# A macaron block on one core: the sample stage in another order, a LayerNorm inside attention, and the third norm beside the output projection

## What is computed

```python
s1, sc1, g1, s2, sc2, g2, s3, sc3, g3 = ada(c)                 # shift, scale, gate per sequence
h = x + 0.5 * g1 * swiglu(modulate(x, g_ffn1, s1, sc1), ...)   # first feed-forward block
z = modulate(h, g_mix, s2, sc2) @ w_in      # conv GLU, q, k, v, index q/k, head weights, two gates
u = glu(z)                                  # prompt: zeros before it; samples: 30 rows of state before it
y = silu(layernorm(depthwise_conv(u, w_dw, 31 taps) + b_dw)) @ w_conv_out
att = sparse_attend(q, top-256 keys by index score) @ w_attn_o # samples: top 65 of 2 cache pages + 4 new keys
h = h + g2 * ((sigmoid(g_c) * y + sigmoid(g_a) * att) @ w_out) # mix and output projection
h = h + 0.5 * g3 * swiglu(modulate(h, g_ffn2, s3, sc3), ...)   # third norm, second feed-forward block
out = rmsnorm(h), k, v, index k, the conv state, for prompt and samples
```

## Time and profile before

| | us |
|---|---|
| median of 3 runs | 2858.69 (2857.79 to 2860.6) |
| profiled execution | 2858.35, its span 2856.2 |
| TensorE busy | 2616.9 (92% of the span) |
| VectorE busy | 1420.9 (50%) |
| ScalarE busy | 595.0 (21%) |
| GpSimd busy | 932.1 (33%) |
| HBM read, written | 172.90 MB, 28.94 MB (71 GB/s) |

### The profile page before, as it was taken

How to read it: one execution, slowest core, us unless ns; L and a number is a source line. 1 busy time by engine, 2 the same in 40 slices (tenths; PEclk the granted TensorE clock), 3 DMA queues, 4 the chain that set the end, 5 groups by cost and what they waited for, 6 DMA issues and landing times.

```text
span 2856.2 us, 42885 instructions
## 1 busy us (share of the span) xinstructions
PE 2616.9 (92%) x15972; PEld 2417.1 (85%) x15972; DVE 1420.9 (50%) x2488; ACT 595.0 (21%) x1064; POOL 932.1 (33%) x493
## 2 busy tenths in 40 slices
PE   5999999999998698989995697998899999999998
PEld 3899999999997487878894335788789999999998
DVE  5333333333337389999999825463343333333333
ACT  3211111111114121123343347510130001011003
POOL 1222222222233156336797001022122233222223
PEclk8999999999999798999997788999999999999999
DMA  7322222222223323211234400143111111111111
GB/s 266 111 74 73 73 73 73 73 73 73 73 64 115 85 68 90 84 37 43 70 102 158 131 15 1 52 129 113 37 31 52 44 44 44 51 44 44 44 44 61
DMA packets 207597, 209.75 MB, mean 73 GB/s; under 512 B 13087, under 2 KB 160659, under 8 KB 206601
## 3 DMA queue, kind: packets, MB, share of 16 engines
q1 hardware_dynamic: 197324, 181.57, 20.2%
q10 hardware_dynamic: 10181, 26.90, 2.9%
HBM read 172.90 MB, written 28.94 MB: 71 GB/s over the span
## 4 chain that ended last, share of the span: by engine, by line
PE 68%; DVE 19%; issue 5%; ACT 3%; SPq 2%; DMA 2%; DVEq 1%; POOL 0%; ACTq 0%; POOLq 0%
PE main L243 20%; PE main L244 20%; PE main L245 19%; DVE top L1264 6%; DVE pick L1277 5%; SPq L1458 2%; DVE pick L1251 2%; PE main L1654 1%; PE aux L483 1%; PE main L1671 1%; PE aux L1682 1%; PE aux L331 1%; DMA out<-kst 1%; PE main L1631 1%; DVE mixt L1969 1%
## 5 line engine op out<-in xcount | busy, mean ns | idle before, releaser
L243 PE MATMUL main<-nhi,whi 128*128 128x352 f32 (+1 forms) x3288 | 1078.7, 328 | 27.8 <-DVE nlo L542 11.8
L244 PE MATMUL main<-nlo,whi 128*128 128x352 f32 (+1 forms) x3288 | 1065.3, 324 | 0.0
L245 PE MATMUL main<-nhi,wlo 128*128 128x352 f32 (+1 forms) x3288 | 1064.4, 324 | 0.0
L232 POOL CAST whi<-raw 128x1024 fp32r<-128x1024 f32 x189 | 202.9, 1074 | 1555.0 <-PE main L245 1205.9
L243 PEld LDWEIGHTS main<-nhi,whi 128*128 128x128 f32 (+1 forms) x3288 | 625.4, 190 | 57.7 <-issue 40.4
L244 PEld LDWEIGHTS main<-nlo,whi 128*128 128x128 f32 (+1 forms) x3288 | 626.4, 191 | 0.7 <-issue 0.2
L245 PEld LDWEIGHTS main<-nhi,wlo 128*128 128x128 f32 (+1 forms) x3288 | 624.5, 190 | 0.5
L234 POOL TENSOR_TENSOR wlo<-raw,whi 128x1024 fp32r<-128x1024 f32 x189 | 476.2, 2519 | 15.2
L761 DVE TENSOR_TENSOR tmp<-main,tmp 128x352 f32<-128x352 f32 x132 | 69.2, 525 | 779.6 <-PE main L245 776.6
L780 DVE SCALAR_TENSOR_TENSOR h<-main,ada,h 128x352 f32<-128x352 f32 (+1 forms) x528 | 296.6, 568 | 114.8 <-PE main L245 114.8
L243 PE MATMUL main<-hid_hi,whi 128*128 128x352 f32 x1056 | 342.6, 324 | 0.0
(11 more groups left out here) (264 smaller groups left out, 2363.4 us busy)
## 6 DMA issues: line engine op xcount, KB each, us to landing
ada_raw<-in_w_ada SPq DMA_DIRECT2D x18, 2048.0 KB, 8.6
raw<-in_w_gate SPq DMA_DIRECT2D x44, 512.0 KB, 3.9
raw<-in_w_up SPq DMA_DIRECT2D x44, 512.0 KB, 3.8
raw<-in_w_down SPq DMA_DIRECT2D x44, 512.0 KB, 3.6
raw<-in_w_in SPq DMA_DIRECT2D x40, 512.0 KB, 3.8
gate_d<-zraw ACTq DMA_DIRECT2D x16, 528.0 KB, 2.7
gates<-gate_d SPq DMA_DIRECT2D x16, 528.0 KB, 4.8
zsw<-zraw ACTq DMA_DIRECT2D x50, 132.0 KB, 2.5
```

Of the source, the lines that this page charges most:

```text
L232: pool.tensor_copy(whi[:, slot], raw[:, slot]).then_inc(hi_done, 1)
L243: pe.matmul(bank, whi[:, slot, w], hi(c), start=(i == 0), stop=False)
L244: pe.matmul(bank, whi[:, slot, w], lo(c), start=False, stop=False)
L245: last = pe.matmul(bank, wlo[:, slot, w], hi(c), start=False, stop=(i == n - 1))
```

## The change

**Sample stage.** TensorE turns the state rows first, then pages, makes the logits of sequences 0 and 1, turns the nine value chunks (through banks 2 and 3 of `main` and both of `aux`), makes the logits of sequences 2 to 7 and turns the keys last. SyncE issues key pages 4 and 5 ahead of the value load, key pages 6 and 7 behind it, and the value pages once the nine value chunks are turned. The copies of new keys and queries go from DVE to ScalarE (ten instead of sixteen), the memset of `qb` to POOL. ScalarE takes the two softmax exponentials inside its loop over the key chunks, at chunks 4 and 5; a third staging row `ksts` is added. DVE takes the maxima between tap 25 and tap 26. The sample value products are issued round the four groups of 32 columns.

**LayerNorm.** Its sums go into attention rounds 0 to 2, the sums of squares into rounds 3 to 5 (each pair in one bank of `main`: 1, 3, 5); the means are subtracted at n = 3, 5, 7, squared at n = 4, 6, 8, and the roots taken at n = 20. TensorE waits for the roots in round `LN_END`.

**Decode convolution.** One product of 992 elements for each channel group, over a view in which the four new positions overlap, and one bias add for all four. `pick` is cleared at the start of `m1_dve`.

**Output projection and third norm.** The first four output tiles are made tile by tile, the other four chunk by chunk, from weight places of their own (`out_hi`, `out_lo`), and wait for the mix by chunk. The third norm is `norm_late` with its steps between the projection's parts; both halves of the squares are on ScalarE.

```diff
@@ z stage: moved from behind the rotated rows to the start of m1_dve
+            dve.memset(pick[:, :], 0.0).then_inc(idx_set, 1)
+            dve.wait_ge(idx_set, 1)
+            for b in range(8):
+                dve.tensor_copy(pick[:, off(b) + P * b:off(b + 1)], cst[:, C_CAUSAL:C_CAUSAL + P]).then_inc(idx_set, 1)
@@ decode convolution
-                for new in range(SNEW):
-                    dve.tensor_tensor(conv_p[:, :, new, :], uext_s[:, c, :, new:new + CW],
-                                      taps[:, c, :].unsqueeze(1).to_broadcast([P, NSEQ, CW]), ALU.mult)\
...
-                dve.tensor_scalar(ys_, ys_, par[:, ROW_BDW + c:ROW_BDW + c + 1], None, ALU.add).then_inc(cv, 1)
+                u = uext_s[:, c, :, 0:CW]
+                shifted = bass.AP(u.tensor, u.offset, [list(u.ap[0]), list(u.ap[1]), [1, SNEW], [1, CW]])
+                dve.tensor_tensor(conv_p[:, :, :, :], shifted,
+                                  taps[:, c, :].unsqueeze(1).unsqueeze(1).to_broadcast([P, NSEQ, SNEW, CW]), ALU.mult)\
...
+            dve.tensor_tensor(conv_y[:, :, SEQ:TOK], conv_y[:, :, SEQ:TOK],
+                              par[:, ROW_BDW:ROW_BDW + 4].unsqueeze(2).to_broadcast([P, 4, NSAMP]), ALU.add)\
...
-        CV_DEC = 4 * 6
+        CV_DEC = 4 * 2 + 1
@@ m2_sp
+            for b in range(4, 6):
+                sp.wait_ge(kp_t, 2 * (b - 3))
+                keys_of(b)
             sp.wait_ge(cv_sum, NPROD)
             sp.dma_start(vraw[:, :, :], v_d).then_inc(v_in, 16)
...
-            sp.wait_ge(kv_t, 18)
+            for b in range(6, NSEQ):
+                sp.wait_ge(kp_t, 2 * (b - 3))
+                keys_of(b)
+            sp.wait_ge(kv_t, 9)
             for b in range(4):
                 values_of(b)
@@ m2_pool
+            pool.wait_ge(acc_done, ZDONE)
+            pool.memset(qb[:, :, :, :], 0.0).then_inc(qb_set, 1)
...
+                    pool.wait_ge(mix_lo, 2 + 3 * KD)
+                    split(pool, T, T % RING, turn(T), ACC_OUT, out_hi[:, m - OUT_RING], out_lo[:, m - OUT_RING])
@@ m2_pe
+            for b in range(2):
+                turn_pages(b)
...
+            for b in range(2):
+                sample_logits(b)
+            pe.wait_ge(u_e, 2)
+            pe.wait_ge(v_in, 16)
+            for t in range(9):
+                turn_tokens(t, vraw, t)
+            for b in range(2, NSEQ):
+                sample_logits(b)
+            for t in range(9):
+                turn_tokens(9 + t, ka, t)
...
+            for half in range(2):
+                pe.wait_ge(vp_in[half], 32 * 4)
                 for k in range(2):
...
+                    for i in range(4):
+                        pe.matmul(main[32 * i:32 * i + 32, (3, 0)[half], :], pts[:, half, k, bass.ts(i, 32)],
+                                  vpg[4 * half + i][:, k, :], start=(k == 0), stop=False, skip_group_check=True)
...
+                if u == LN_END:
+                    pe.wait_ge(ln_sem["sd"], 3)
...
+                if u < NTC:
+                    ln_mean(u)
+                elif u < 2 * NTC:
+                    ln_squares(u - NTC)
...
+            for p, (m, t) in enumerate(OUT):
+                pe.wait_ge(split_done, T_OUT + m + 1)
+                if m == 0:
+                    pe.wait_ge(mix_lo, 2 + 3 * (KD - 1) + t + 1)
...
+                if p in SUMS_AFTER:
+                    norm_3["sums"](pe, SUMS_AFTER.index(p))
...
+        SUMS_AFTER = (17, 21)
@@ m2_act
+            act.wait_ge(k_in, 16)
+            for i in range(2):
+                act.activation(kts[:, i, :, PAST:SKEYS], ka[:, :, SEQ:TOK], ACT.Copy).then_inc(sa_q, 1)
...
+                if t in (4, 5):
+                    half = t - 4
+                    act.wait_ge(ss, 8 * half + 2)
+                    act.activation(ls[:, half, :], main[:, 4 + half, 0:SKEYS], ACT.Exp, bias=nb[:, half:half + 1],
...
+                if n == 2 * H + 4:
+                    act.wait_ge(split_done, T_MIX + 3)
+                    for t in range(NTC):
+                        act.wait_ge(ln_sem["mm"], t + 1)
+                        act.activation(rstd_c[t][:, :], main[:, 2 * t + 1, 0:TC], ACT.Sqrt, scale=1.0 / D_CONV, bias=eps)\
@@ m2_dve
-            conv_taps(dve, 16, CW)
+            conv_taps(dve, 16, 26)
...
+            conv_taps(dve, 26, CW)
...
+                for step, *at in DVE_NORM3.get(p, ()):
+                    norm_3[step](dve, *at)
...
+        DVE_NORM3 = {17: (("inverse", 0),), 18: (("scale", 0, 0),), 19: (("scale", 0, 1),), 20: (("low", 0, 0),),
+                     21: (("low", 0, 1),), 22: (("inverse", 1),)}
@@ third norm: what is left behind the last part, on ScalarE and on DVE
+            squares(2)
+            act.wait_ge(out_free, 9 + 3 * KD)
...
+            m["affine"](act, 1, 1)
+            m["root"](act, 2)
+            m["affine"](act, 2, 0)
+            m["affine"](act, 2, 1)
...
+            m["scale"](dve, 1, 0)
+            m["scale"](dve, 1, 1)
+            m["low"](dve, 1, 0)
+            m["inverse"](dve, 2)
+            m["low"](dve, 1, 1)
+            m["scale"](dve, 2, 0)
+            m["scale"](dve, 2, 1)
+            m["low"](dve, 2, 0)
+            m["low"](dve, 2, 1)
@@ SyncE's order of stages
+            ffn2["sp"](sp)
             g_row_load(sp)
-            ffn2["sp"](sp)
```

More of the change, by code:

```diff
@@ L1394, in build @@
         pts4 = [place("pt", [P, 2, 8, P], F32, UB + 33792), place("pt_n", [P, 2, 8, P], F32, NB + 58368)]
-        kst = place("kst", [P, 2, ATT], F32, UB + 33792)
+        ksts = [place(f"kst{i}", [P, ATT], F32, (UB + 33792, UB + 35840, NB + 65536)[i]) for i in range(3)]
         ust = place("ust", [NSAMP, 2, D_CONV], F32, UB + 37888)
@@ L1435, in build @@
         LN_AT = 36
+        LN_END = 2 * H - 1
         def lb_of(n):
@@ L1585, in m2_pe @@
                     turn_pages(b + 2)
+            pe.wait_ge(glu, 12)
+            for c in range(4):
+                last = pe.transpose(main[0:HIST, 2, bass.ts(c, P)], uext[:, c, SEQ:SEQ + HIST], ident)
+            last.then_inc(u_t, 1)
+            for c in range(4):
+                last = pe.transpose(main[0:NSAMP, 3, bass.ts(c, P)], unew[:, c, :], ident)
+            last.then_inc(u_t, 1)
+            for b in range(2):
+                turn_pages(b)
+            pe.wait_ge(tk, TK_SAMPLE)
+            for half in range(2):
+                pe.matmul(main[:, 4 + half, 0:SKEYS], cst[0:NSAMP, C_SELT + P * half:C_SELT + P * (half + 1)],
+                          pick_s[:, :], start=True, stop=False, skip_group_check=True)
+            pe.wait_ge(sa_q, 2 + H)
+            for b in range(2):
[8 more added lines that the diff above has]
+                turn_tokens(9 + t, ka, t)
             def ln_mean(t):
@@ L1786, in m2_act @@
                     .then_inc(u_out, 16)
-            for b in range(2, NSEQ):
-                copy_pages(b)
-            for half in range(2):
-                act.wait_ge(ss, 8 * half + 2)
-                act.activation(ls[:, half, :], main[:, 4 + half, 0:SKEYS], ACT.Exp, bias=nb[:, half:half + 1],
-                               scale=HD ** -0.5, accum_out=sums[:, 0, half:half + 1]).then_inc(se, 1)
+            act.wait_ge(k_in, 16)
+            for i in range(2):
+                act.activation(kts[:, i, :, PAST:SKEYS], ka[:, :, SEQ:TOK], ACT.Copy).then_inc(sa_q, 1)
@@ new lines, in m2_act @@
+            for b in range(4, NSEQ):
+                copy_pages(b)
+            for t in range(9):
+                n = P if t < 8 else NSAMP
+                dst = ksts[t % 3][0:n, :]
+                act.wait_ge(kv_t, 9 + t + 1)
+                if t >= 3:
+                    act.wait_ge(kst_out[t % 3], 16 * (t // 3))
+                act.activation(dst, turn_bank(9 + t)[0:n, :], ACT.Copy).then_inc(kv_e, 1)
+                act.wait_ge(kv_e, 9 + t + 1)
+                act.dma_start(out[2][0, 0, t * P:(t + 1) * P].rearrange("t h d -> t (h d)") if t < 8 else
+                              out[6][0].rearrange("b s h d -> (b s) (h d)"), dst).then_inc(kst_out[t % 3], 16)
+                if t in (4, 5):
+                    half = t - 4
+                    act.wait_ge(ss, 8 * half + 2)
+                    act.activation(ls[:, half, :], main[:, 4 + half, 0:SKEYS], ACT.Exp, bias=nb[:, half:half + 1],
+                                   scale=HD ** -0.5, accum_out=sums[:, 0, half:half + 1]).then_inc(se, 1)
@@ L1810, in m2_act @@
                 .then_inc(so_e, 1)
-            act.wait_ge(kst_out[0], 16 * 5)
-            act.wait_ge(kst_out[1], 16 * 4)
+            for t in range(3):
+                act.wait_ge(kst_out[t], 16 * 3)
             def turned(n):
```

270 lines of the change are left out of this document (114 added, 156 removed).

## The result

The changed kernel takes 2806.43 us (median of 4, 2803.39 to 2809.0) against 2858.24 for the kernel before in the same comparison: a ratio of 0.9819 [0.9802, 0.9836], 51.8 us less. The forecast was 2805. The profiled execution has a span of 2805.3 us, 50.9 less than before.

The account below looks back on a forecast made before the run. TensorE, 92% busy, gains only where it idles or runs at the lower clock, before the second feed-forward block. Terms -48.7 + 17.2 - 8.4 - 13.6 = -53.5 take 2858.35 to 2805 us; range 2796 to 2814.

Parts of the forecast that it names:

- Clearing the scores: DVE, z stage: moving the memset and eight causal copies into idle time gains 4.4 us (bounds 0 and 5.4).
- Decode convolution: DVE, sample stage: four 992-element products and one bias add make it 16 us instead of 24.3 (bounds 10 and 19.5).
- SyncE: Sample stage page loads: 2.65 us a page, queries land at 1552.0, last value page is in at 1617.
- DVE meanwhile: Sample stage taps: ten slow, 40 fast to 1603.6; last ends at 1618.6, within 2 us of the page chain.
- Sample values: TensorE before attention: overlapping column groups take 1.9 + 0.9 us per half, not 11.2; attention starts near 1626.
- LayerNorm in attention: Attention: six sums moved in cost 15.0 + 2, roots 3.5, clock gives back 4; sum +17.2 us (bounds +8, +34).
- Projection: Output projection: waiting for the mix by chunk removes the 7.43 us wait and more, -8.4 (bounds -6 and -9.5).
- third norm: After the projection: 31 us from last part to chunk 2's product instead of 54.6, -13.6 (bounds -9 and -16).
- the first: Rival: TensorE stays at 1.2 GHz in early attention, LayerNorm there costs +34, time 2822 us; chance 0.13.
- the second: Rival: column groups in the sample value products do not overlap, each half stays 11.2 us, time 2815; chance 0.10.
- the third: Rival: cheaper, decode convolution near 10 us and LayerNorm partly in gaps, -6 and -8, time 2791; chance 0.14.
- the fourth: Rival: slower than before, DVE's taps stay beside POOL at 2.16 us more each, up to 2912; chance 0.03.

Follow-up runs that it names:

- e8: The changed kernel with the clearing of `pick` and its eight causal copies put back in front of the first scores: 2812.39 us, ratio 0.9830 to the kernel before.
- e2: The changed kernel with the sixteen page numbers read into SyncE registers once, ahead of the stage: 2800.22 us, ratio 0.9794 to the kernel before.
- e1: The changed kernel with POOL's three weight splits for the mix waiting for the last convolution tap: 2805.22 us, ratio 0.9813 to the kernel before.
- e11: The changed kernel with fifteen unread products added on TensorE around its waits in the sample stage: 2805.93 us, ratio 0.9810 to the kernel before.
- e6: The changed kernel with attention's three LayerNorm square roots replaced by scalings without a root (timing only): 2803.46 us, ratio 0.9810 to the kernel before.
- e9: The changed kernel with all eight output projection tiles made tile by tile, the third norm's finer steps kept: 2821.38 us, ratio 0.9870 to the kernel before.
- e5: The changed kernel with the sample value products issued sequence by sequence, not round the four column groups: 2819.83 us, ratio 0.9857 to the kernel before.

## Why the prediction was right, step by step

The total was right to 1.4 us, but partly because errors cancelled.

- *Clearing the scores* (4.4): borne out within some 2 us, the spread of e8's one profile (4.4) and of its time (3.1 to 6.0). But of the 3.1 us of cover that the prediction counted none was left: the eight copies took 4.74 us in the new place, and the rotation starts 1.3 later.
- *Decode convolution* (16 us): 13.45. The product of 992 elements was taken near the disturbed end; its rows are 1.18 once and 2.06 three times, and the bias add 1.16.
- *SyncE*: the last value page is in at 1617.12, forecast 1617, though the chain began 4.6 earlier. The working lacked that a page number read right behind a load of 2 MB takes far longer: SyncE issues nothing from 1535.67 to 1542.03 and from 1555.12 to 1562.50, while in e2, where no number is read there, the next page load follows at 1535.34. In the second gap 0.4 us are a wait for turned pages. Only part of this is on the path (the queries land meanwhile), but the value pages start at 1574.2 instead of 1572. So 1617 came out by two errors that cancelled, the early start and the slow reads.
- *DVE meanwhile*: maxima at 1599.5 (forecast 1603.6), last tap at 1615.1 (1618.6), each about as much too early as the decode convolution (4.6). "Two chains end within 2 us" is what e1 and e2 show.
- *Sample values* (2.8 a half): 4.9 and 5.5. The step that failed is the row it was priced by: the adaLN products' 1.90 were at full speed, these run at 1.2 GHz after TensorE had waited 10.84 us for the softmax. e11 gives 1.92 at the higher clock. Only the second half lies behind the last page, so 2.7 us of this are on the path; from its end to attention it took 5.2, forecast 6.
- *LayerNorm in attention* (+17.2): +14.1. The six sums take 17.6 (forecast 17), the first 4.91 at the lower clock, the others 2.5. Round by round the kernel is 10.8 behind the pace of before once the six sums are done and 9.0 after nine rounds, where the terms of the forecast make 13.7 (17 + 2 - 4 - 1.3): the full speed that comes earlier, and perhaps sums that lie in gaps, give back more than the 4 put down for it; no run separates the two. The roots then cost 4.0, and another 1.1 a round later, 5.1 where 3.5 was forecast; e6 shows that 4.1 of it are the table loads and the clock behind them. The attention that follows loses nothing more.
- *Projection* (-8.4) and *third norm* (-13.6): -7.4 and -12.2. The first is read from the trace alone. e9 shows that the order of the parts carries the second. The 33.4 us behind the last part hold two scales that take 4.61 us together, the first beside the end of a split on POOL (1.61 each elsewhere in this norm), which the sum did not have.
- *The rest* (0): +1.5. In the 10 us behind chunk 2's first product the granted clock is 0.83, and 53 products run where 63 ran before.

Of the rivals, the first did not come (1.00 from 8.4 us on), the second is excluded by e5, the third came in part (the decode convolution), and the fourth needed POOL to work beside DVE for 84 us more; its splits ended at 1554.2.

## What to carry to other kernels

Where a stage ends on two chains, shorten each alone and both together: e1 by itself is worth nothing that the runs can tell, and shortening both shows the third thing that waits. A row is a price only at its clock: look at the granted clock of the stretch it comes from and at what TensorE did before the stretch it is used for. A number that an engine reads from memory to issue a DMA belongs in a register ahead of the stage; here that was 6 us (7 by the ratios) for an edit of a few lines.

## What the runs showed of the hardware that was not expected

- SyncE's read of a page number and the issue of its load take 2.3 to 2.6 us; the issue alone 0.6 to 0.8. Right behind the issue of loads of 2 MB the first such pair comes only after 6.4 and 7.4 us (0.4 of the second is a wait for turned pages).
- A convolution tap on DVE takes 1.27 us alone and 3.36 beside POOL; POOL's subtraction of a split takes 2.34 alone and 3.20 beside the taps, its cast 1.04 and up to 2.03. The Trainium skill, SBUF — State Buffer, SBUF: two separate sides, says that a DVE instruction with two inputs in SBUF and a GpSimd instruction that reads SBUF hold their shared port for a whole instruction, and the other is blocked. By that rule each would wait for the other in turn, and the trace agrees: both get longer, and 1.27 + 2.34 = 3.6 for one of each in turn, an estimate, is near the 3.36 and 3.20.
- Four column groups give the work of four in the time of one: 16 records in 1.92 us (e11) against 4 in 1.90 (e5), both at full speed, a factor of 4.0. The Trainium skill, TensorE: Matmul & The Clock Gate, Measured speedup vs the span model, has 2.38 for three such groups; no run here used three.
